# Feed-forward gate and up: one hi block against both operand halves in a 512-column product

## The reference

```python
def conv_ffn(hn, w_up, conv_w, conv_b, w_down):          # the first one, "ffn_c"
    u = causal_dwconv(hn @ w_up, conv_w) + conv_b        # three taps over positions
    gate, val = jnp.split(u, 2, axis=-1)
    return (jax.nn.silu(gate) * val) @ w_down

def swiglu(h, w_gate, w_up, w_down):                     # the other four, "ffn_0" to "ffn_3"
    return (jax.nn.silu(h @ w_gate) * (h @ w_up)) @ w_down
```

## Time and profile before

| | us |
|---|---|
| three runs, median (lowest to highest) | 1983.32 (1982.18 to 1983.72) |
| the profiled execution: span from first to last instruction | 1978.7 |
| busy TensorE / weight loads / VectorE / ScalarE / GpSimd | 1823.4 / 1761.0 / 1211.8 / 835.0 / 135.7 |
| matmuls | 14226 |

### The profile page before, as it was taken

The page is one execution under the profiler, slowest core; times in us unless marked ns, Lnnn a source line. Parts: engine busy times, 40 slices in busy tenths (PEclk is TensorE's granted clock), DMA queues, the critical chain, the costliest instruction groups (busy, mean ns, idle before and its releaser), DMA issues.

```text
span 1978.7 us, 33445 instructions
## 1 busy us (share of the span) xinstructions
PE 1823.4 (92%) x14226; PEld 1761.0 (89%) x14226; DVE 1211.8 (61%) x1244; ACT 835.0 (42%) x808; POOL 135.7 (7%) x79
## 2 busy tenths in 40 slices
PE   7997989889889998999999799998899999899996
PEld 7985989789889998999997699998799986799995
DVE  5676545486458887655665655555655576565564
ACT  4555212154343344443554454336444352453344
POOL 2000000021010000100101110002100010010002
PEclk9997989899899998999997899999899997899998
DMA  7432221435334443445542045553355532155441
GB/s 267 169 120 99 81 75 59 137 127 202 115 128 170 173 173 142 166 176 189 180 176 107 7 151 193 189 181 138 132 184 175 188 138 75 52 188 175 186 170 43
DMA packets 42595, 286.86 MB, mean 145 GB/s; under 512 B 4656, under 2 KB 6832, under 8 KB 9104
## 3 DMA queue, kind: packets, MB, share of 16 engines
q1 hardware_dynamic: 38480, 273.70, 38.5%
q0 software_dynamic: 2800, 10.69, 1.5%
q10 hardware_dynamic: 1232, 1.25, 0.2%
HBM read 281.42 MB, written 4.19 MB: 144 GB/s over the span
## 4 chain that ended last, share of the span: by engine, by line
PE 78%; DVE 10%; ACT 4%; POOL 4%; issue 2%; DMA 1%; DVEq 0%; ACTq 0%; POOLq 0%
PE PS L374 78%; POOL arena L273 4%; DVE arena L1476 3%; ACT arena L1000 2%; DVE ring_lo L1473 1%; DVE arena L1473 1%; ACT ring_hi L1000 1%; DVE operand_lo L1528 1%; DMA arena<-in_mem_t 1%; ACT L1000 1%; ACT operand_hi L1000 0%; DVE residual L1473 0%; DMA ring_raw<-in_w_stream 0%; DVE arena L1612 0%; DVE arena L1607 0%
## 5 line engine op out<-in xcount | busy, mean ns | idle before, releaser
L374 PE MATMUL PS<-operand_hi,ring_hi 128*128 128x256 f32 x3092 | 895.9, 290 | 48.2 <-DVE operand_lo L1528 33.8
L374 PE MATMUL PS<-operand_lo,ring_hi 128*128 128x256 f32 x3092 | 885.1, 286 | 0.0
L374 PE MATMUL PS<-operand_hi,ring_lo 128*128 128x256 f32 x3092 | 884.4, 286 | 0.0
L1473 DVE TENSOR_TENSOR ring_lo<-ring_raw,ring_hi 128x2048 fp32r<-128x2048 f32 x260 | 613.0, 2363 | 317.2 <-ACT ring_hi L1000 316.8
L374 PEld LDWEIGHTS PS<-operand_hi,ring_hi 128*128 128x128 f32 x3092 | 604.1, 195 | 55.7 <-issue 19.5
L1000 ACT ACTIVATE ring_hi<-ring_raw 128x2048 fp32r<-128x2048 f32 x260 | 493.8, 1905 | 282.4 <-PE PS L374 277.0
L374 PEld LDWEIGHTS PS<-operand_lo,ring_hi 128*128 128x128 f32 x3092 | 604.2, 195 | 2.3 <-issue 1.7
L374 PEld LDWEIGHTS PS<-operand_hi,ring_lo 128*128 128x128 f32 x3092 | 603.5, 195 | 0.0
L374 PE MATMUL PS<-hidden_hi,ring_hi 128*128 128x256 f32 x880 | 249.1, 283 | 1.3 <-DVE hidden_lo L1473 1.3
L374 PE MATMUL PS<-hidden_lo,ring_hi 128*128 128x256 f32 x880 | 249.0, 283 | 0.0
L374 PE MATMUL PS<-hidden_hi,ring_lo 128*128 128x256 f32 x880 | 249.0, 283 | 0.0
(11 more groups left out here) (160 smaller groups left out, 1121.4 us busy)
## 6 DMA issues: line engine op xcount, KB each, us to landing
ring_raw<-in_w_stream SPq DMA_DIRECT2D x260, 1024.0 KB, 4.8
spilled_gates<-arena POOLq DMA_DIRECT2D x12, 256.0 KB, 2.3
arena<-spilled_gates POOLq DMA_DIRECT2D x2, 1536.0 KB, 9.6
tables<-in_tables POOLq DMA_DIRECT2D x1, 1344.0 KB, 10.9
residual<-in_x_t ACTq DMA_DIRECT2D x4, 256.0 KB, 5.9
arena<-in_mem_t POOLq DMA_DIRECT2D x1, 1024.0 KB, 13.3
out_t<-residual SPq DMA_DIRECT2D x1, 1024.0 KB, 4.5
arena<-in_spatial_t POOLq DMA_DIRECT2D x1, 512.0 KB, 3.6
```

What stands on the lines that cost most here:

```text
L374: return nc.tensor.matmul(out, lhs, rhs, start=start, stop=stop, skip_group_check=True)
L1473: return v.tensor_tensor(out, a, b, op)
```

## The change

`XH` and `XL` become the two halves of one tensor `X2`, so that hi and lo of operand tile k can be given as one moving operand of 2 x 256 columns. In the feed-forward's gate and up slabs the new `wide_slab` replaces `output_slab`: a hi block meets both halves in one matmul of 512 columns, which fills a whole bank (first half hi x hi, second half hi x lo), and the lo block meets the hi half in one of 256 columns, added to the first half. That is 32 matmuls a slab instead of 48, over the same number of columns, and an output tile now takes a bank instead of half of one. Gate takes banks 0 and 1, up banks 2 and 3, down banks 4 to 7. The down slabs and all other stages keep their three matmuls a block.

The two halves are added on the way out: ScalarE copies the second half of both banks to SBUF (`gate_copy`, `up_copy`), VectorE adds the first half (`gate_sum`, `up_sum`), and then scales in SBUF. TensorE waits for these sums (`halves_added`) before it fills the banks again. In ffn_c the first tap goes from VectorE to ScalarE (`last_tap`: Identity with scale and bias from memory), and VectorE waits for it (`conv_begun`).

The norm's sum comes behind slab two instead of in its middle. It still goes to bank 7, which is now one of the down banks: the zero product of bank 7 waits for `norm_root`. The norm between ffn_c and ffn_0 sums in bank 0, that of `per_layer` in bank 3, and `per_layer` copies four adjacent banks in one instruction instead of two. Three semaphores of the rwkv part are merged in one. The core of the diff:

```diff
-        XH = sb("operand_hi", [P, 20, T], F32R)
-        XL = sb("operand_lo", [P, 20, T], F32R)
+        X2 = sb("operand", [P, 2, 20, T], F32R)
+        XH, XL = X2[:, 0], X2[:, 1]
...
+            def wide_slab(g0, first, i=0, by=3, fresh=()):
+                slot, _, g = place(g0, i, by)
+                pe.wait_ge(lo_split, g + 1)
+                for m in range(2):
+                    out = bank(first + m)
+                    for k in range(KT):
+                        if m == 0 and k in fresh:
+                            operands(1)
+                        w = slice((m * KT + k) * P, (m * KT + k + 1) * P)
+                        mm(out.rearrange("p (s t) -> p s t", s=2), ring_hi[:, slot, w], X2[:, :, k, :], k == 0, False)
+                        last = mm(out[:, 0:T], ring_lo[:, slot, w], XH[:, k, :], False, k == KT - 1)
+                last.then_inc(multiplied, 1)
...
-                output_slab(g0, 0, bank(0), fresh=EVERY)
-                output_slab(g0 + 1, 0, bank(1), between=norm_sum)
-                for b in range(3, 7):
+                wide_slab(g0, 0, fresh=EVERY)
+                wide_slab(g0 + 1, 2)
+                norm_sum()
+                for b in range(4, 8):
+                    if b == 7:
+                        pe.wait_ge(sem("norm_root"), norms[0])
                     for m in range(2):
                         mm(bank(b)[:, m * T:(m + 1) * T], zeros[:, 0:P], zeros[:], True, False)
                 with pe.Fori(0, FP // 2) as i:
-                    pe.wait_ge(gate_scaled, i * 2 + (n * FP + 1))
-                    output_slab(g0 + 2, 0, bank(2), i, 6)
-                    pe.wait_ge(sem("norm_root"), norms[0])
-                    pe.wait_ge(up_taken, i * 2 + (n * FP + 1))
-                    output_slab(g0 + 3, 0, bank(7), i, 6)
-                    down(g0 + 4, 0, i, i * 2 + (n * FP + 1))
-                    pe.wait_ge(gate_scaled, i * 2 + (n * FP + 2))
-                    output_slab(g0 + 5, 0, bank(0), i, 6)
-                    pe.wait_ge(up_taken, i * 2 + (n * FP + 2))
-                    output_slab(g0 + 6, 0, bank(1), i, 6)
-                    down(g0 + 7, 1, i, i * 2 + (n * FP + 2))
+                    for odd in range(2):
+                        pe.wait_ge(sem("halves_added"), i * 4 + (2 * n * FP + 1 + 2 * odd))
+                        wide_slab(g0 + 2 + 3 * odd, 0, i, 6)
+                        pe.wait_ge(sem("halves_added"), i * 4 + (2 * n * FP + 2 + 2 * odd))
+                        wide_slab(g0 + 3 + 3 * odd, 2, i, 6)
+                        down(g0 + 4 + 3 * odd, odd, i, i * 2 + (n * FP + 1 + odd))
...
+                def last_tap(acc, x, tile_):
+                    for m in range(2):
+                        last_ = run(acc[:, m, :], x[:, m, :], ACT.Identity,
+                                    scale=prm[:, bass.ds(tile_ + (m + COL["ffn_conv_w"] + 2 * 4 * FP), 1)],
+                                    bias=prm[:, bass.ds(tile_ + (m + COL["ffn_conv_b"]), 1)])
+                    last_.then_inc(sem("conv_begun"), 1)
+                gate_in, up_in = conv_x if conv else (tiled(silu_out), tiled(hidden))
+                def second_half(out, first):
+                    sides = bank(first, 2).rearrange("p (m s t) -> p m s t", m=2, s=2)
+                    run(out, sides[:, :, 1, :]).then_inc(sem("half_copied"), 1)
+                def gate_copy(at, i, pair):
+                    act.wait_ge(multiplied, place(at, i, 6)[2] + 1)
+                    act.wait_ge(up_taken, pair + (n * FP + 1))
+                    second_half(gate_in, 0)
+                def up_copy(at, i, pair):
+                    act.wait_ge(multiplied, place(at, i, 6)[2] + 1)
+                    if at > START["ffn_c"] + 1:
+                        act.wait_ge(sem("hidden_lo"), pair + n * FP)
+                    second_half(up_in, 2)
+                def gate_tap(pair):
                     if conv:
-                        if split is not None:
-                            split_slab(split, i, 6)
+                        act.wait_ge(gate_scaled, pair + 1)
+                        last_tap(conv_acc, conv_x[0], pair * 2)
...
+                gate_copy(g0, 0, 0)
                 split_slab(g0 + 3)
+                up_copy(g0 + 1, 0, 0)
                 norm_root()
+                gate_tap(0)
                 gate(0)
+                up_tap(0)
                 up(0, 0)
                 with act.Fori(0, FP // 2) as i:
-                    split_slab(g0 + 4, i, 6)
-                    gate(i * 2 + 1, i, g0 + 5)
-
-                    up(i * 2 + 1, 1, i * 6 + (g0 + 2))
-                    split_slab(g0 + 6, i, 6)
-                    split_slab(g0 + 7, i, 6)
-                    gate(i * 2 + 2, i, g0 + 8)
-                    up(i * 2 + 2, 0, i * 6 + (g0 + 5))
-                    split_slab(g0 + 9, i, 6)
+                    for odd in (1, 0):
+                        pair = i * 2 + (2 - odd)
+                        split_slab(g0 + 7 - 3 * odd, i, 6)
+                        gate_copy(g0 + 5 - 3 * odd, i, pair)
+                        gate_tap(pair)
+                        split_slab(g0 + 8 - 3 * odd, i, 6)
+                        if not conv:
+                            gate(pair)
+                        up_copy(g0 + 6 - 3 * odd, i, pair)
+                        if conv:
+                            gate(pair)
+                            up_tap(pair)
+                            split_slab(g0 + 9 - 3 * odd, i, 6)
+                        up(pair, odd, i * 6 + (g0 + 5 - 3 * odd))
+                        if not conv:
+                            split_slab(g0 + 9 - 3 * odd, i, 6)
...
+                def add_halves(out, first, copies):
+                    dve.wait_ge(sem("half_copied"), copies)
+                    sides = bank(first, 2).rearrange("p (m s t) -> p m s t", m=2, s=2)
+                    return tt_(out, out, sides[:, :, 0, :], ALU.add)
+                def gate_sum(pair):
+                    add_halves(gate_in, 0, pair * 2 + (2 * n * FP + 1)).then_inc(sem("halves_added"), 1)
+                def gate_scale(pair):
+                    dve.wait_ge(sem("halves_added"), pair * 2 + (2 * n * FP + 1))
+                    mul(gate_in, gate_in, factor()).then_inc(gate_scaled, 1)
...
-                    for m in range(2):
-                        w2 = prm[:, bass.ds(tile_ + (m + COL["ffn_conv_w"] + 2 * 4 * FP), 1)]
-                        b = prm[:, bass.ds(tile_ + (m + COL["ffn_conv_b"]), 1)]
-                        v.tensor_scalar(acc[:, m, :], x[:, m, :], w2, b, ALU.mult, ALU.add)\
-                         .then_inc(sem("conv_tap"), 1)
-                    dve.wait_ge(sem("conv_tap"), before + 2)
...
+                gate_sum(0)
                 split_slab(g0 + 3)
+                up_sum(0)
                 norm_factor()
-                gate(g0, 0, 0, 0)
-                up(g0 + 1, 0, 0, 0, 1)
+                gate_scale(0)
+                up_scale(0)
+                gate(0)
+                up(0, 0)
                 with dve.Fori(0, FP // 2) as i:
-                    split_slab(g0 + 4, i, 6)
-                    gate(g0 + 2, i, i * 2 + 1, 2, g0 + 5)
-                    up(g0 + 3, i, i * 2 + 1, 1, 7)
-                    split_slab(g0 + 6, i, 6)
-                    split_slab(g0 + 7, i, 6)
-                    gate(g0 + 5, i, i * 2 + 2, 0, g0 + 8)
-                    up(g0 + 6, i, i * 2 + 2, 0, 1)
-                    split_slab(g0 + 9, i, 6)
+                    for odd in (1, 0):
+                        pair = i * 2 + (2 - odd)
+                        split_slab(g0 + 7 - 3 * odd, i, 6)
+                        gate_sum(pair)
+                        gate_scale(pair)
+                        if conv:
+                            gate(pair)
+                        split_slab(g0 + 8 - 3 * odd, i, 6)
+                        if not conv:
+                            gate(pair)
+                        up_sum(pair)
+                        up_scale(pair)
+                        up(pair, odd)
+                        split_slab(g0 + 9 - 3 * odd, i, 6)
...
```

## The result

The kernel after takes **1986.97 us** (median of 20 runs, 1983.68 to 1992.95) against 1980.84 of the kernel before beside it (20 runs, 1974.36 to 1989.52): a ratio of 1.0037, 95% interval 1.0027 to 1.0046. That is 6 us slower, and the forecast was 8 us faster. The profiled execution spans 1987.9 us, 9.2 more than the one of before.

A forecast was written before the change was run, and what follows sets the result against it. TensorE bounds the kernel, with VectorE to become the bound in ffn_c. Fusion -16.1, starts -2.2, ffn_c +8.9 and clock +1.5 sum to -7.9, from 1983.3 to 1975.4 us; range 1958 to 1986.

The forecast's parts named there:

- The fused product: Gate and up slabs of ffn_0 to ffn_3: one 0.2274 us matmul replaces two totalling 0.240, saving 16.1 us.
- The bounds 0.2133 and 0.240: Limits for a fused matmul's time: 0.2133 us for columns alone (18.0 us more saved), 0.240 with nothing saved.
- Rival 2: Matmul costs by column, or the operand's second run eats the saving: +8.2, 1991.5 us; chance 0.14 shared with rival 4.
- Rival 4: The 512-column matmuls are cut in two on the way, outcome like rival 2; chance 0.14 shared with it.
- Cover in ffn_0 to ffn_3: The added copies and sums, about 1.4 us a pair on VectorE, fit beside TensorE, which stays the bound.
- VectorE's round in ffn_c: VectorE becomes ffn_c's bound at 17.8 us a pair against TensorE's 16.88, costing 8.9 us.
- rival 1: TensorE stays the bound in ffn_c too, no clock lost: -23.7, 1959.6 us; chance 0.20.
- the handover of the tap: VectorE's wait in ffn_c for ScalarE's tap: 1.07 us for both Identities, 1.13 with the semaphores.
- Rival 3: ffn_c's round exceeds 18.2 because ScalarE comes late with a tap: at 18.7 us, 1983 us, no change; chance 0.11.
- The clock: TensorE's idle of about 4.5 us in ffn_c lowers its clock, costing 1.5 us, bounds 0 and 3.
- The starts: Norm's sum moved behind slab two: -2.4 in ffn_0 and ffn_2, +1.5 in ffn_1, +1.1 in ffn_3, together -2.2 us.
- 0.72 for faster: Chance given to a time below 1979.4 us; slower, above 1987.3, had 0.13, and the same 0.15.

The follow-up runs named there:

- experiment 3: Kernel after with hi and lo of each operand tile side by side, so the 512 columns are one contiguous run: 1987.12 us, 1.0035 times the kernel before.
- experiment 2: Kernel after with two products of 256 columns instead of the fused one, from the second of eight blocks on: 1992.64 us, 1.0067 times the kernel before.
- experiment 8: Kernel after with ScalarE taking the norm's root and its table load ahead of the copy of the up's half: 1983.39 us, 1.0017 times the kernel before.
- experiment 6: Kernel after with ffn_c's next up slab split before the gate's tap on ScalarE, and during it on VectorE: 1971.60 us, 0.9959 times the kernel before.
- Experiments 9 and 10: 9: kernel after, norm's sum back in the middle of slab two, root first, 1986.34 us. 10: kernel before, VectorE's second split waiting for GpSimd's folds, 1975.18 us.
- experiment 11: Kernel after with gate tap behind the split, eight wide products then eight narrow per output tile, root before copy: 1966.62 us, 0.9927 times the kernel before.

## Why the prediction was wrong

The sign was wrong. The mechanisms were named, two of the three places came out as told, but each term of the sum that was to gain was put too large and each that was to lose too small: +7.1 in the fusion, +1.2 in the starts, +3.7 in ffn_c, +1.0 in the clock. -7.9 + 13.0 = +5.1 us.

**The fused product** (step "I take 0.2274"). This is the largest miss. The rows of 512 columns stand in a run of their own kind; between products of 256 columns the pair takes 0.353, not 0.347. The saving of 0.0126 halves to 0.0067, 16.1 us to 9.0. The bounds 0.2133 and 0.240 held it, at 0.233 by the rest of the pair. Rival 2 put the point from which the change loses at 0.2336, by its own sum, and that is nearly where it fell. Its mechanism, a second run that costs something, is refuted by experiment 3, and a matmul doesn't cost by column alone either (experiment 2). Rival 4 falls too: matmuls of 512 columns stand in the timeline, and their number in all falls by 14226 - 12466 = 1760, which is 16 in each of 110 gate and up slabs. By an estimate from the fixed part of 2.5 ns (the Trainium skill, "TensorE: Matmul & The Clock Gate", Back-to-back issue gap) the saving would be 3.2 us. The measured 9.0 lies between that and mine: I had put the rule aside on two pure runs, where what counts here is the mixed one.

**Cover in ffn_0 to ffn_3.** Right: no idle of TensorE in the loop, though two copies and two sums came in.

**VectorE's round in ffn_c.** The mechanism is right, rival 1 is refuted, and the first down slab came at 603.6 on the old clock (606.18 less the 2.55 by which the stage begins later), where 603.5 was forecast. The round was to be 17.8 and is 18.15. The term that failed is the handover of the tap, 0.03 us a semaphore, for which the prediction names no row: the four here cost 0.14 to 0.24 each. The earlier trace rows had a hint of it, 0.15 and 0.19 us of idle where VectorE waits for nothing but its own last instruction. The sum before a scale was 0.16 shorter than put in (0.72, not 0.88), and that hid part of it. 9 x 0.35 makes 3.2 of the 3.7 us. TensorE's idle of 0.9 a pair came nearly as told, 0.86, which is in part luck: VectorE's round was longer by 0.35 and TensorE's three slabs by 0.19, and the two errors work against each other. Rival 3's cause, ScalarE late by a split or a copy, is not what happened: ScalarE was idle for 3.92 and 2.94 us before its taps. But its price, a longer round, is the direction in which the forecast fell.

**The clock.** Idle before the last down slab 4.5 forecast, 4.37 measured; the slab after it took 2.45 more, inside the bounds of 0 and 3. The row that I took the 1.5 from was a shorter wait with clock 0.58 over 3.5 us. Here the clock was 0.50 over the first 4 us of the slab and 0.81 over the next 4, and 2.45 us lost at half pace make 4.9 us at 0.50. The idle before it does not set the loss by itself: in the kernel of experiment 8 the same slab came after 4.47 us of idle and took 7.21, in that of experiment 6 after 2.15 us and took 7.18.

**The starts.** -2.4 in ffn_0 and ffn_2 was forecast, -1.7 and -2.35 came; +1.5 and +1.1 in ffn_1 and ffn_3, +1.7 and +1.4. So the sizes are near, and the reason was wrong. I credited the move of the sum with the cover of GpSimd's folds. Experiments 9 and 10 show that the folds were 2 us longer only because VectorE split a second slab beside them, and that in the kernel after another edit had ended this. The move is a cover only where that split still comes early, as in experiment 6's kernel. The question missed was why three folds take 8.47 us in one stage and 4.57 in another.

**The chances.** 0.72 for faster stood on one price from a pure run, and on a round that was a sum of ten small numbers with nothing added for what a new handover costs. The range, 1958 to 1986, ended 1 us short, since rival 2 was left outside it and its price and the losses of ffn_c were not let vary together. Even that 1 us flatters it: the range was built on a median of 1983.3 from three runs, and with the 1980.84 of twenty the same range would end at 1983.5, 3.5 us short.

**What stays open.** What decides whether a slab runs at 0.353 or at 0.347 a pair. Some slabs of the same code in the same stage differ, and a slab keeps its pace to the end. And why ffn_c's loop stays above the kernel before's 182.41 even in experiment 11 (186.11): TensorE waits 7.4 us in three waits there, two in the first 30 us of the loop and one at the last down slab, against 3.5 in two before, and the last down slab takes 7.21 instead of 5.71. Why the early waits are longer I did not take apart.

## What to carry to other kernels

Work that moves from the engine that bounds to an idle one pays only if the first engine has something else to do until the result is back: 1.08 us of VectorE's time (1.77 less the scale's 0.69) became 1.47 us of waiting here, and with a split in between at the gate's tap the kernel is 15 us faster, by the medians, than the one as changed. The price of an instruction form in a run of its own kind is not its price between others, so a gain of a few ns times a thousand needs a mixed row or wide bounds. Where the same operation has two durations in one trace, look at what the other engines do beside it before the wait behind it is credited to an order.

## What the runs showed of the hardware

- A product of 512 columns took 0.2274 us in a run of its own kind, 0.230 in runs of eight, and alternating with products of 256 columns the two together took 0.353 (most slabs) or 0.346 to 0.347, where the pure prices add up to 0.347. Whether the 512 columns are one run or two changes nothing.
- At 1.2 GHz the fusion saves nothing. In the start of ffn_1 in the kernel of experiment 8 the clock was 0.50, and two wide products with a narrow one between them lie 0.64 apart, three times the 0.213 between products of 256 columns after ffn_c's last wait:

```profile
1177.53 0.63 PE L377 MATMUL PS<-operand,ring_hi 128*128 128x512 f32 x1
...
1178.17 0.63 PE L377 MATMUL PS<-operand,ring_hi 128*128 128x512 f32 x1
```

- GpSimd's adds and VectorE's subtraction of two SBUF operands hold each other up: the three folds take 4.57, 6.5 or 8.4 to 8.5 us with none, one or two splits beside them (experiments 9 and 10). A split that starts while a fold runs takes up to 2.8 instead of 2.29 us; the one that starts just before the third fold takes 2.29, and the fold ends 0.59 us behind it. The Trainium skill ("GPSIMD Engine Reference", 1. Specifications) says that the two engines share their ways to SBUF and contend when VectorE reads two inputs there; the traces agree, with about 1.9 us for each split.
- A handover between VectorE and ScalarE around an Identity whose scale and bias are addressed by a register cost 0.14 to 0.24 us each way.
- The root follows its table load by 0.01 us here too (1180.23 + 1.28 = 1181.51, root at 1181.52).
